# Attention outputs that come out turned: V as the stationary operand, and local units with two heads of each key

## What is computed

```python
q_a, k_a, v_a, q_b, k_b, v_b, q_idx, k_idx, w_idx, c_q, c_kv, k_rope = split_cols(x @ w_in)
o_a = sliding_window_sink_attn(q_a, k_a, v_a, sinks)        # 8 query heads of 64, 2 key heads, window 128
o_b = indexer_sparse_attn(q_b, k_b, v_b, q_idx, k_idx, w_idx)   # 4 heads of 64, one key head, best 64 keys
o_c = mla_attn(...)                                         # 4 heads, values of 64, causal
y = concatenate([o_a, o_b, o_c])                            # 512 + 256 + 256 = 1024 columns
x = layer_norm(alpha * x + y @ w_out) ; then router, 16 experts, layer_norm
```

## Time and profile before

| | |
|---|---|
| time, median of 3 runs | 1146.23 us (1144.69 to 1147.26) |
| span of the profiled execution | 1143.1 us |
| TensorE busy | 1096.5 us (96%) |
| VectorE busy | 890.5 us (78%) |
| ScalarE busy | 746.8 us (65%) |
| mean granted clock of TensorE | 0.995 of full speed |

### The profile page before, as it was taken

The page is one execution under the profiler, slowest core; times in us unless marked ns, Lnnn a source line. Parts: engine busy times, 40 slices in busy tenths (PEclk is TensorE's granted clock), DMA queues, the critical chain, the costliest instruction groups (busy, mean ns, idle before and its releaser), DMA issues.

```text
span 1143.1 us, 14686 instructions
## 1 busy us (share of the span) xinstructions
PE 1096.5 (96%) x5515; PEld 910.4 (80%) x5515; DVE 890.5 (78%) x1476; ACT 746.8 (65%) x1325; POOL 0.2 (0%) x4
## 2 busy tenths in 40 slices
PE   7899999999999999999999999999989999999996
PEld 5688888888787788888878787887778878787774
DVE  4756757777768867766678869999976886999996
ACT  5746565655666665577465557888846655688883
POOL 0000000000000000000000000000000000000000
PEclk9999999999999999999999999999999999999998
DMA  8654454453443455634552417999926331599991
GB/s 293 229 200 147 147 184 140 159 180 111 147 146 113 161 207 165 215 111 138 160 182 74 148 40 238 350 369 359 359 73 239 112 119 66 174 359 362 353 369 40
DMA packets 131843, 221.26 MB, mean 194 GB/s; under 512 B 6144, under 2 KB 77360, under 8 KB 131760
## 3 DMA queue, kind: packets, MB, share of 16 engines
q1 hardware_dynamic: 127920, 213.21, 54.8%
q10 hardware_dynamic: 3840, 6.98, 1.8%
HBM read 219.13 MB, written 1.05 MB: 193 GB/s over the span
## 4 chain that ended last, share of the span: by engine, by line
PE 77%; DVE 12%; ACT 6%; issue 2%; DMA 2%; ACTq 0%; DVEq 0%
PE bank L489 21%; PE bank L491 20%; PE bank L490 20%; PE bank L852 3%; PE bank L788 3%; DVE wL L442 2%; ACT wH L434 1%; PE bank L638 1%; DMA ring<-in_w_mem_kv 1%; PE bank L837 1%; PE bank L2275 1%; PE bank L2324 1%; ACT S L811 1%; PE bank L1736 1%; PE bank L2289 1%
## 5 line engine op out<-in xcount | busy, mean ns | idle before, releaser
L442 DVE TENSOR_TENSOR wL<-ring,wH 128x1024 fp32r<-128x1024 f32 (+1 forms) x316 | 375.6, 1212 | 128.4 <-ACT wH L434 127.1
L434 ACT ACTIVATE wH<-ring 128x1024 fp32r<-128x1024 f32 (+1 forms) x316 | 320.4, 1047 | 32.0 <-PE bank L491 15.0
L489 PE MATMUL bank<-wH,hTH 128*128 128x512 f32 (+2 forms) x592 | 235.8, 398 | 3.2 <-DVE wL L442 2.3
L491 PE MATMUL bank<-wH,hTL 128*128 128x512 f32 (+2 forms) x592 | 229.5, 388 | 0.0
L490 PE MATMUL bank<-wL,hTH 128*128 128x512 f32 (+2 forms) x592 | 229.4, 388 | 0.0
L489 PEld LDWEIGHTS bank<-wH,hTH 128*128 128x128 f32 x592 | 111.8, 189 | 26.1 <-DVE wL L442 4.5
L491 PEld LDWEIGHTS bank<-wH,hTL 128*128 128x128 f32 x592 | 111.5, 188 | 21.8
L490 PEld LDWEIGHTS bank<-wL,hTH 128*128 128x128 f32 x592 | 111.8, 189 | 20.0 <-issue 0.5
L489 PE MATMUL bank<-wH,xgH 128*128 128x512 f32 x256 | 104.4, 408 | 0.0
L491 PE MATMUL bank<-wH,xgL 128*128 128x512 f32 x256 | 100.3, 392 | 0.0
L490 PE MATMUL bank<-wL,xgH 128*128 128x512 f32 x256 | 99.9, 390 | 0.0
(11 more groups left out here) (296 smaller groups left out, 1849.1 us busy)
## 6 DMA issues: line engine op xcount, KB each, us to landing
ring<-in_w_in_a SPq DMA_DIRECT2D x44, 1024.0 KB, 5.1
ring<-in_w_out SPq DMA_DIRECT2D x20, 1024.0 KB, 4.9
ring<-in_w_down SPq DMA_DIRECT2D x20, 1024.0 KB, 6.9
ring<-in_w_gate SPq DMA_DIRECT2D x36, 512.0 KB, 5.3
ring<-in_w_up SPq DMA_DIRECT2D x36, 512.0 KB, 6.8
ring<-in_w_in_b SPq DMA_DIRECT2D x14, 1024.0 KB, 5.1
ring<-in_w_mem_kv SPq DMA_DIRECT2D x8, 1024.0 KB, 7.1
ring<-in_w_in SPq DMA_DIRECT2D x8, 1024.0 KB, 5.3
```

What stands on the lines that cost most here:

```text
L434: act.e.activation(quarter_parts(q)[0], quarter_in_ring(q), COPY).then_inc(w_high, 1)
L442: dve.e.tensor_tensor(lo, quarter_in_ring(q), hi.bitcast(F32), SUB).then_inc(w_low, 1)
L489: pe.e.matmul(o, a[0], b[0], start=first, stop=False)
L491: return pe.e.matmul(o, a[1], b[0], start=False, stop=last)
```

## The change

V becomes the stationary operand and PT moves (`pe_values_turned`): the output has the head's 64 columns on the partitions and the tokens along the row. Two heads go to partitions 0 to 63 and 64 to 127 of the same bank (the two column halves of the array). One over the sum lies per token on the partitions and must now run along the row: TensorE multiplies the column, spread to 64, by the identity (four products more a unit, into the other half of the bank), ScalarE copies the result to Y (`act_one_over`), VectorE multiplies (`dve_turned_emit`). Y then already holds the turned tile; ScalarE copies the high part (`act_y_high`) and VectorE subtracts (`dve_y_low`), once for each unit and with no transposes. The local units take two heads of each key head, so their scores use both row halves and always two banks. The chunks of w_out are read in the order that this gives.

```diff
-        four = by_rows(t["w_out_2"][l], 0) + by_rows(t["w_out_2"][l], 4)
-        slab(f"p{l}0", 1024, [four[3], four[0]])
-        slab(f"p{l}1", 1024, [four[1], four[2]])
+        slab(f"p{l}0", 1024, two_chunks(t["w_out_2"][l], 6, 7) + two_chunks(t["w_out_2"][l], 0, 2))
+        slab(f"p{l}1", 1024, two_chunks(t["w_out_2"][l], 1, 3) + two_chunks(t["w_out_2"][l], 4, 5))
...
+        def y_ready(label, k, i):
+            if label[0] == "o":
+                return at("yT", label, k - k % 2)
+            l = int(label[1])
+            return at("yT", (("C", l, i), ("W", l, 0, i), ("W", l, 1, i), ("S", l, i))[k // 2])
...
-            pe.wait_ge(at("yT", label, k - k % 2))
             for i in range(2):
+                pe.wait_ge(y_ready(label, k, i))
...
+        def pe_values_turned(u):
+            b = bank_of["turn", u.name, 0]
+            r = small(4, "r", u.name)
+            pe.wait_ge(*u.v_ready)
+            for kt in range(u.nk):
+                pe.wait_ge(at("PT", u.name, kt))
+                for c, pair in enumerate(u.pairs):
+                    for n, s in enumerate(pair):
+                        mm = pe.e.matmul(b.t[64 * n:64 * n + 64, c * P:(c + 1) * P], u.vh(s, kt), u.PT[:, kt, s, :],
+                                         start=kt + c == 0, stop=kt == u.nk - 1, skip_group_check=True)
+            pe.wait_ge(at("one over sum", u.name))
+            for c, pair in enumerate(u.pairs):
+                for n, s in enumerate(pair):
+                    mm = pe.e.matmul(b.t[64 * n:64 * n + 64, 256 + c * P:256 + (c + 1) * P], r[:, s:s + 1].to_broadcast([P, 64]), ident,
+                                     start=True, stop=True, skip_group_check=True)
+            mm.then_inc(*pe.did("values", u.name))
+
+        def dve_turned_emit(u):
+            b = bank_of["turn", u.name, 0].t
+            dve.wait_ge(at("shares kept", u.name))
+            dve.follow().tensor_tensor(mix_output(u), b[:, 0:256], mix_output(u), MUL).then_inc(*dve.did("emit", u.name))
+
+        def act_one_over(u):
+            act.wait_ge(at("values", u.name))
+            act.e.activation(mix_output(u), bank_of["turn", u.name, 0].t[:, 256:512], COPY).then_inc(*act.did("shares kept", u.name))
...
         def act_run(units, between, behind_scores=nothing):
...
                 act_exp(u)
+                if n and units[n - 1].pairs:
+                    act_one_over(units[n - 1])
                 between(2 * n)
                 between(2 * n + 1)
             act_turn(units[-1])
+            if units[-1].pairs:
+                act_one_over(units[-1])
             between(2 * len(units))
 
         def dve_run(units, between, behind_scores=nothing):
             for n, u in enumerate(units):
                 dve_max(u)
                 dve_sink(u)
+                if n and units[n - 1].pairs:
+                    dve_one_over_sum(units[n - 1])
                 behind_scores(n)
                 between(2 * n)
                 if n:
                     units[n - 1].emit(units[n - 1])
                 between(2 * n + 1)
+            if units[-1].pairs:
+                dve_one_over_sum(units[-1])
             between(2 * len(units))
             units[-1].emit(units[-1])
...
+        def act_y_high(u):
+            act.wait_ge(at("emit", u.name))
+            act.e.activation(y_part(u)[0], mix_output(u).rearrange("p (c n) -> p c n", c=2), COPY).then_inc(*act.did("high", "yT", u.name))
+
+        def dve_y_low(u):
+            high, low = y_part(u)
+            dve.wait_ge(at("high", "yT", u.name))
+            dve.e.tensor_tensor(low, mix_output(u).rearrange("p (c n) -> p c n", c=2), high.bitcast(F32), SUB).then_inc(*dve.did("yT", u.name))
...
+            windowed = [Unit(("W", l, x, i), i, i + 1, lambda s, x=x: qT[s // 2 * 64:s // 2 * 64 + 64, 2 * x + s % 2, :], lambda s: kT[s // 2 * 64:s // 2 * 64 + 64, 0, :],
...
+                             sink=sinks[:, x, :, :], n_banks=2, pairs=((0, 1), (2, 3)), chunk=2 + 2 * x) for x in range(2) for i in range(2)]
...
-        OUT_AT = {5: (0, 2, 2), 9: (2, 2, 4)}
+        OUT_AT = {5: 4, 9: 6}
...
+                if n % 2 == 1 and n > 1:
+                    act_y_high(others[n // 2 - 1])
...
+            for u in latent:
+                dve_y_low(u)
             dve_upto(f"p{l}0", 2)
...
                 if n == 4:
                     best_mask(1)
+                if n > 1:
+                    dve_y_low(others[n - 2])
 
             def between(n):
                 if n == 12:
-                    dve_flip_y_tile(f"p{l}", 6, 0)
+                    dve_y_low(others[4])
                 if n % 2 == 1 and n > 1 or n == 12:
                     dve_ahead(1)
```

More of the change, by code:

```diff
@@ L761, in write, with __init__ @@
         class Unit:
-            def __init__(self, name, i, nk, qh, kh, vh, dv, scale, mask, mx, den, emit, ready, v_ready, sink=None, k0=0, n_banks=None):
+            def __init__(self, name, i, nk, qh, kh, vh, dv, scale, mask, mx, den, emit, ready, v_ready, sink=None, k0=0, n_banks=None, pairs=None, chunk=0):
                 self.name, self.i, self.nk, self.qh, self.kh, self.vh, self.dv, self.scale, self.mask = name, i, nk, qh, kh, vh, dv, scale, mask
@@ L765, in __init__ @@
                 self.n_banks = n_banks or nk
+                self.pairs, self.chunk = pairs, chunk
                 parity[0] ^= 1
@@ L828, in dve_one_over_sum @@
                 dve.follow().tensor_tensor(u.den, u.den, small(4, "es", u.name), ADD).then_inc(*dve.did())
-            dve.follow().reciprocal(r, u.den).then_inc(*dve.did())
+            dve.follow().reciprocal(r, u.den).then_inc(*dve.did("one over sum", u.name))
             return r
@@ L958, in dve_flip_y, with y_part, mix_output @@
                 dve.e.tensor_tensor(low, o, high.bitcast(F32), SUB).then_inc(*dve.did("yT", label, j0))
[L962 to L981, removed]
+        def y_part(u):
+            return [z[:, u.chunk:u.chunk + 2, u.i * P:(u.i + 1) * P] for z in yT2]
+        def mix_output(u):
+            a = 128 * u.chunk
+            return Y[:, u.i, a:a + 256]
+        def act_y_high(u):
[5 more added lines that the diff above has]
+            dve.e.tensor_tensor(low, mix_output(u).rearrange("p (c n) -> p c n", c=2), high.bitcast(F32), SUB).then_inc(*dve.did("yT", u.name))
         def dve_gated(label, n):
@@ L1672, in index_units @@
                          [at("qI", l, 0), at("kI", l, 0)], None, n_banks=2) for i in range(2)]
-        def dve_by_pairs(i):
-            def emit(u):
-                r = dve_one_over_sum(u)
-                y = Y[:, i, 512:768].rearrange("p (b a d) -> p a b d", a=2, b=2)
-                dve.wait_ge(at("values", u.name))
-                for x in range(2):
-                    dve.follow().tensor_tensor(
-                        y[:, x, :, :], bank_of["turn", u.name, 0].t[:, 128 * x:128 * x + 128].rearrange("p (b d) -> p b d", b=2),
-                        bc(r[:, 2 * x:2 * x + 2].unsqueeze(2), [P, 2, 64]), MUL).then_inc(*dve.did("emit", u.name))
-            return emit
@@ L1756, in pe_mix_layer @@
             latent, others = mix_units(l)
-            def outputs(a, n, at_):
-                pe_flip_y(f"p{l}", at_, n, lambda i, j: Y[:, i, (a + j) * P:(a + j + 1) * P], at("emit", {6: latent[1], 0: others[1], 2: others[3], 4: others[5]}[a].name))
             def between(n):
@@ L1991, in dve_mix_layer @@
             dve_run(latent, between)
-            dve_flip_y(f"p{l}", 0, 2)
+            for u in latent:
+                dve_y_low(u)
             dve_upto(f"p{l}0", 2)
@@ L2011, in between @@
                 if n in OUT_AT:
-                    dve_flip_y(f"p{l}", OUT_AT[n][2], 2)
-                    dve_upto(f"p{l}0", OUT_AT[n][2] + 2)
+                    dve_upto(f"p{l}0", OUT_AT[n])
             dve_run(others, between, behind_scores)
-            dve_flip_y_tile(f"p{l}", 6, 1)
+            dve_y_low(others[5])
             dve.q = end(f"p{l}1")
```

46 lines of the change are left out of this document (19 added, 27 removed).

## The result

The changed kernel takes **1162.33 us** (median of 4 runs, 1161.00 to 1164.03) against 1145.51 of the kernel before (4 runs, 1144.69 to 1147.26): 1.0105 times as long, 95% interval 1.006 to 1.015. The quotient of these two medians is 1.0147: the ratios in this text, each with its interval, aren't the quotients of the medians. The profiled execution of the changed kernel took 1163.57 us, 1162.2 of them span. The 1.4 us around the span are 1.3 to 1.5 in every execution that has both numbers; the 3.1 that I had read off compare a median with the profile of another, quicker execution. Run again in later rounds, the same kernel took 1162.46 us (6 runs; ratio 1.0106, interval 1.0065 to 1.0146). So it is slower, by 1 to 1.5%.

What follows compares the result with a forecast made beforehand. TensorE was taken as the bound, but barely, with VectorE a hidden second bound up to 3.5 us behind. Four places summed to 7.2 us a layer, 14.4 for two: 1146.2 + 14.4 = 1160.6 us, 80% range 1152 to 1174.

Steps and rivals of the forecast that it cites:

- Place 3: Output chunk 2: TensorE stands 2.9 us for a low part late in VectorE's queue; +3.3 us a layer.
- Place 1: Latent units: ScalarE waits for values before cutting weights, delaying VectorE's low part and the first local scores; +1.4 us a layer.
- the two terms (1.4 and 1.3, twice): Delays from ScalarE's weight cuts standing behind the shares, in the latent units (+1.4) and the tail (+1.3), each layer.
- The rival that the cuts hide: ScalarE's late weight cuts cost nothing because VectorE finds slack: 4.5 us a layer, 1155 us; chance 0.13.
- Place 2: Up to the end of the last local unit's scores: shorter scores and other savings outweigh new waits; -0.6 us a layer.
- Place 4: The rest of the layer after chunk 2: values, chunk 4's wait for a low part (+1.35), the tail (+1.3).
- The values: TensorE's value products with stationary V: 1.4 us for 16 records, 1.9 for 24; 3.2 us a layer more.
- the lower bound: Values in column halves run beside each other like the chosen units' row halves: 0.66 us for 8 records.
- The clock: Rival: stands bring TensorE's granted clock down, 3 to 4 us of work a layer at half clock; 1168 us, chance 0.07.
- Halves in series: Rival: column halves run one after the other, 1.08 us for each 8 records; +6.8 a layer, 1174 us, chance 0.15.
- VectorE keeps up: Rival: low parts are there when asked for, TensorE's balance alone stands; -3.1 us a layer, 1140 us, chance 0.05.
- TensorE's balance: TensorE's own work: transposes -1.6, their waits -2.1, local scores -2.6, values +3.2; -3.1 us a layer.

Runs made afterwards that it cites:

- e1: Changed kernel with two of VectorE's low parts a layer moved ahead of the next maxima: 1149.80 us, ratio 1.0019.
- e2: Changed kernel with ScalarE cutting its weights before it waits for the values and copies the shares: 1157.10 us, ratio 1.0071.
- e8: Changed kernel with both two low parts a layer ahead of the maxima and ScalarE's weight cut before the shares: 1145.94 us, ratio 0.9971.
- e3: Changed kernel with VectorE taking one over the sum of the previous unit before the maxima of the next: 1166.16 us, ratio 1.017.
- e4: Kernel before with only the regrouped local units (two heads of each key, two banks), outputs still turned by transposes: 1153.97 us, ratio 1.0024.
- e10: The changed kernel run again without any edit, in later rounds: 1162.46 us, ratio 1.0106.
- e5: Changed kernel with twelve idle TensorE products filling the wait before the second half of output chunk 2: 1158.79 us, ratio 1.01.

## Why the prediction was right

It forecast 1160.6 us from 14.4 us of loss; the two layers lost 15.4, the kernel 16.8 by its medians. The mechanism is the one forecast, low parts late in VectorE's queue. That the number is so close is in part luck: the terms are further off than the sum. How far each layer is behind the kernel before, counted from the mask of C0, gives the cost of each place (us):

| place | forecast | layer 0 | layer 1 |
|---|---|---|---|
| 1, to the mask of W00 | +1.4 | +0.8 | +0.8 |
| 2, to the end of W11's scores | -0.6 | +0.3 | +0.1 |
| 3, to the end of chunk 2 | +3.3 | +3.9 | +5.0 |
| 4, to the router's transposes | +3.1 | +2.8 | +1.7 |
| together | 7.2 | 7.8 | 7.6 |

In layer 1 the clock stays at 1.00 up to chunk 2 and is low only in its second half (2.86 us where that takes 1.43), so there place 3 is 3.5 of waits and work and 1.4 of clock. Point by point:

- *Place 3* is right: 3.5 us at the full clock in both layers, against 3.3. The wait is 3.29 and 3.31 us instead of 2.9. e1 shows the cause, and that VectorE's order and not its speed makes this wait.
- *Place 1* was charged 1.4 and cost 0.8: W00's mask comes 21.86 us after that of C0 instead of 21.04 (623.13 less 602.09 in the kernel before):

```profile
623.13 0.48 PE L784 MATMUL bank<-maskR,identR 128*128 128x512 f32 x1
```

  e2 shows the mechanism. The order of ScalarE's queue at the head and the tail is worth 5 us over both layers, the two terms (1.4 and 1.3, twice) said 5.4. The rival that the cuts hide is refuted.
- *Place 2* has the wrong sign. It was to give back 0.6 and costs 0.1 to 0.3. The wait for the reciprocal is 1.69 as forecast (1.7), and those for VectorE's multiply are 0.8 and 0.6 in layer 1 (0.8 and 0.4 forecast), but TensorE waits for the exp of W00 for 0.9 us and not 0.35. In layer 0 the waits for the multiply are missing; W10's scores and the turn of W01 ran at the low clock instead (from 635.55 to 638.34, 2.8 us where these steps take 1.5).
- *Place 4* was charged 3.1. The wait of chunk 4 is 0.71 and 0.51 us (+1.35 forecast), the last one 0.95 (+1.3). In layer 0 some 1.2 of its 2.8 us are the low clock behind chunk 2.
- *The values, a term mis-sized.* It was to be 1.4 us for 16 records and 1.9 for 24, and is 1.02 and 1.46. Of the 0.2 us for entering and leaving the halves, charged for each group, the entry shows with 0.1: the product ahead of the values holds the engine for 0.33 us (667.68 to 668.01), where it is 0.22 in the kernel before (660.16 to 660.38); leaving costs nothing that shows. And the lower bound, 0.66 us for 8 records as in the row halves of S, was none: 8 records of values in column halves take 0.49 us to the next group, the 8 of the spread 0.53. Against 0.8 and 1.7 before, the 3.2 us a layer of longer values are, with 0.1 for each entry, 4 x 0.3 more and 4 x 0.14 less, some 0.6. Some of this was hidden anyway, by waits that take it up.
- *The clock* took the place of the values' term. It was a rival with 0.07, as a whole: 1168. It came in part. The product of length and clock is 75.3 and 76.6 us for the layers of the profiled run, so 3.1 and 1.6 us of them are low clock. Without it the layers lose some 4.7 and 6.1, 10.8 together (rather more, since the product takes too much out, as told above), and the sum of 14.4 would have been up to 3.6 us too much. The values charged too high and the clock not charged are errors of opposite sign; the total is closer than its parts. The argument against this rival was a misreading. The window row says 1.00 for the first matmuls after 7.5 us of idleness, but the 16 transposes there take 3.67 us, 0.42 each, where 8 take 1.03 and each 0.27 in layer 0; in the changed kernel, in a window at 0.59, each takes 0.42 too. So they ran at the pace of the low clock, whatever the row says:

```profile
7.80 3.67 PE L638 MATMUL bank<-const,M 128*128 128x128 f32 x16
...
617.88 1.03 PE L638 MATMUL bank<-const,G 128*128 128x128 f32 x8
```

- *Halves in series* is refuted: eight records start within 0.49 us (668.01 to 668.50), where one after the other they would need 1.08. The Trainium skill ("TensorE: Matmul & The Clock Gate", Part 3, The mechanism) says that distinct column groups run together, and the trace agrees. Its rule there that a weight load overlaps a running matmul only where the row group differs does not fit (the same section also lets a load into a background buffer go ahead): the halves share their rows, and their eight loads of 137 ns, 1.1 us if they ran one after the other, are over in 0.42 us and cost the eight matmuls nothing beyond their 0.49.
- *VectorE keeps up* is refuted by the list of waits. But e8 shows that it was one step away: with two reorderings the gain is there, 0.9 us a layer of the 3.1 that TensorE's balance promised. What keeps the rest isn't shown. I take it to be VectorE's load, 57.7 of 69.7 us in layer 0 of e8, in a chain of score, turn and value steps that asks for it at set points; 1.7 us of it is still the wait for the reciprocal, and some of layer 0 is low clock (0.98 on the mean).

What stays open: why the kernel with the reciprocal first (e3) has the lowest clock, what makes the clock fall after one stand and not after another, and whether VectorE's work or only its order keeps e8 from the rest of the gain.

## What to carry to other kernels

When an operand moves from one engine's work to another's, first write down the queue of the engine that must deliver it, with what stands in front, and only then count what the busiest engine saves: here two 0.4 us subtractions in each layer, one of them behind 4.8 us of other work, cost 6 us a layer with the clock that they brought down, and the transposes with their waits had cost 3.7. Put what another engine waits for ahead of what nobody waits for yet; two such edits turned 15 to 17 us of loss into a tie, or a gain of 0.3% at most. And count the buffers that are alive at once when a unit takes one more, since a shorter product that then waits for a bank gained nothing in e4.

## What the runs showed of the hardware

**The clock moves the kernel before as well.** Its time went from 1144.8 to 1156.3 us over 23 runs on one chip while the product of span and clock stayed at 1132.9 to 1138.1. Four of the 23 had 0.983 and some 1156 us. So nearly all the scatter of this unchanged kernel goes with TensorE's granted clock, and a single run of it can be 1% off for no reason in the program.

**The clock falls after short stands, sometimes.** After 3.29 us of waiting it went from 1.00 (2.4 GHz) to 0.52 (nearly all at 1.2 GHz) in 652 to 655 us in one profile, and stayed at 1.00 in the other. Over six such stands in three profiles of turned kernels it fell five times. Behind the 1.7 us wait for the reciprocal, twice each in the changed kernel, e10, e1, e2, e5 and e8, it fell five times of twelve, each time in layer 0. The Trainium skill ("TensorE: Matmul & The Clock Gate", "HAM oscillation") says that idle gaps between bursts bring the clock down: this trace agrees, with the numbers just given.

**The clock's row can be wrong at a kernel's start.** It says 1.00 from 0 us on, where 16 transposes take 0.42 us each; at a granted 1.00 in layer 0 they take 0.27. The length of a known instruction is the check.

**Two column halves, with V stationary, are quicker than V moving.** Eight records of 128 moving columns take 0.49 us from start to start, where eight with 128 stationary and 64 moving columns took 0.81 before (614.22 to 615.03). With the eight that spread 1/sum a tile-1 unit takes 1.46 us where 16 records took 1.73 (636.54 to 638.27), and a tile-0 unit 1.02 instead of 0.81. Going from the full array into the halves costs another 0.1 us for each unit.
